# Toeplitz transfers from the diagonal on, with zeros written early, on the S5 stage of a one-core trunk kernel

## The reference

```
u      : 64 groups of 16 features
states : s[t] = lam_bar * s[t-1] + b_bar u[t]   (complex, 64 states a group)
y      = gelu(real(c s) + d * u)
y      = y * sigmoid(y @ glu_w + glu_b)         (1024 x 1024)
```

## Time and profile before

| what | us |
|---|---|
| median of 3 runs | 1279.68 (1279.62 to 1280.75) |
| the profiled execution | 1278.21 |
| its span | 1276.4 |
| start of the first GLU product in it | 101.61 |
| x load for the transposes: issue by SP, and time to landing | 50.39, 7.6 |
| POOL's last instruction ends | 78.4 |

### The profile page before, as it was taken

The page is one execution under the profiler, slowest core; times in us unless marked ns, Lnnn a source line. Parts: engine busy times, 40 slices in busy tenths (PEclk is TensorE's granted clock), DMA queues, the critical chain, the costliest instruction groups (busy, mean ns, idle before and its releaser), DMA issues.

```text
span 1276.4 us, 16013 instructions
## 1 busy us (share of the span) xinstructions
PE 1240.6 (97%) x6277; PEld 1034.5 (81%) x6277; DVE 671.7 (53%) x785; ACT 462.0 (36%) x486; POOL 64.8 (5%) x82
## 2 busy tenths in 40 slices
PE   3889999999999999999999999999999999999998
PEld 3778888888888888888888888888888888888886
DVE  8997754344444444646655465634454444444443
ACT  5635433333333333333333333422333333332232
POOL 6940000000000000000000000000000000000000
PEclk9999999999999999999999999999999999999999
DMA  5373333332312334323232133233232323323331
GB/s 115 100 144 123 99 99 99 99 99 90 105 58 90 105 90 138 107 66 107 66 99 83 57 107 96 69 96 93 74 119 80 102 94 99 99 68 90 93 110 66
DMA packets 141039, 121.03 MB, mean 95 GB/s; under 512 B 5720, under 2 KB 132880, under 8 KB 141008
## 3 DMA queue, kind: packets, MB, share of 16 engines
q1 hardware_dynamic: 138832, 116.40, 29.5%
q10 hardware_dynamic: 2176, 4.20, 1.7%
HBM read 114.29 MB, written 2.10 MB: 91 GB/s over the span
## 4 chain that ended last, share of the span: by engine, by line
PE 94%; ACTq 2%; ACT 2%; DMA 1%; DVE 1%; issue 0%; SPq 0%; DVEq 0%
PE bank L709 27%; PE bank L711 27%; PE bank L710 27%; PE bank L809 2%; PE bank L808 2%; PE bank L807 2%; ACTq L434 2%; DMA s<-in_x_dram 1%; PE bank L835 1%; PE bank L837 1%; PE bank L836 1%; PE bank L846 1%; PE bank L820 0%; PE bank L821 0%; ACT s_states L900 0%; PE bank L537 0%
## 5 line engine op out<-in xcount | busy, mean ns | idle before, releaser
L709 PE MATMUL bank<-u_hi,w_hi 128*128 128x512 f32 x960 | 374.9, 391 | 0.0
L711 PE MATMUL bank<-u_hi,w_lo 128*128 128x512 f32 x960 | 373.6, 389 | 0.0
L710 PE MATMUL bank<-u_lo,w_hi 128*128 128x512 f32 x960 | 373.5, 389 | 0.0
L1186 DVE TENSOR_TENSOR w_lo<-w_raw,w_hi 128x2048 fp32r<-128x2048 f32 x112 | 256.4, 2290 | 165.7 <-ACT w_hi L900 165.6
L900 ACT ACTIVATE w_hi<-w_raw 128x2048 fp32r<-128x2048 f32 x112 | 214.0, 1910 | 319.1 <-PE bank L711 314.0
L709 PEld LDWEIGHTS bank<-u_hi,w_hi 128*128 128x128 f32 x960 | 180.2, 188 | 37.8 <-issue 0.7
L710 PEld LDWEIGHTS bank<-u_lo,w_hi 128*128 128x128 f32 x960 | 180.2, 188 | 37.6 <-issue 0.5
L711 PEld LDWEIGHTS bank<-u_hi,w_lo 128*128 128x128 f32 x960 | 180.2, 188 | 37.5
L709 PE MATMUL bank<-h_hi,w_hi 128*128 128x512 f32 x352 | 136.9, 389 | 0.0
L710 PE MATMUL bank<-h_lo,w_hi 128*128 128x512 f32 x352 | 136.9, 389 | 0.0
L711 PE MATMUL bank<-h_hi,w_lo 128*128 128x512 f32 x352 | 136.9, 389 | 0.0
(11 more groups left out here) (220 smaller groups left out, 1321.6 us busy)
## 6 DMA issues: line engine op xcount, KB each, us to landing
w_raw<-in_ret_w_qkvg_dram SPq DMA_DIRECT2D x24, 1024.0 KB, 4.9
w_raw<-in_ffn_w_gate_dram SPq DMA_DIRECT2D x22, 1024.0 KB, 5.2
w_raw<-in_ffn_w_up_dram SPq DMA_DIRECT2D x22, 1024.0 KB, 5.1
w_raw<-in_ffn_w_down_dram SPq DMA_DIRECT2D x32, 704.0 KB, 4.1
w_raw<-in_ret_w_o_dram SPq DMA_DIRECT2D x8, 1024.0 KB, 5.1
w_raw<-in_s_glu_w_dram SPq DMA_DIRECT2D x4, 1024.0 KB, 5.5
s<-in_x_dram ACTq DMA_DIRECT2D x8, 256.0 KB, 8.5
s_w<-in_x_dram SPq DMA_DIRECT2D x1, 2048.0 KB, 7.6
```

The costliest lines, as they stand in the source:

```text
L709: pe.matmul(o, w_hi[w][:, w_cols], hi, start=first, stop=False)
L710: pe.matmul(o, w_hi[w][:, w_cols], lo, start=False, stop=False)
L711: return pe.matmul(o, w_lo[w][:, w_cols], hi, start=False, stop=end)
L1186: dve.tensor_tensor(w_lo[s][:, :], w_raw[:, s, :], w_hi[s][:, :].bitcast(F32), ALU.subtract).then_inc(w_lo_ready[s], 1)
```

## The change

Seven edits, all of them in the S5 stage:

- `strip` lies in the second half of `w_raw` only and holds the eight steps; sixteen partitions of the first half hold zeros (one memset by POOL).
- A Toeplitz transfer for r writes only the steps from r on: 8 - r steps instead of 8. The number of transfers stays.
- Seven transfers by SP, for r = 1 to 7, write the zeros of all parts and both halves, 16 partitions x 8 x r steps, from when the last transpose of `xn` is done.
- SP issues GLU piece 0 right after these have landed and the x load is issued, before its first Toeplitz part; piece 1 when all parts have landed.
- ACT splits piece 0 between the gelu table load and `strip_out(7)`.
- PE: `y_inputs(4)` before `y_states(0, 0)`; transposes 0 to 3 behind `y_inputs(7)`.
- `s5_input_out` goes through chunk, real or imaginary, j, with j innermost: it writes four floats in a row and reads PSUM with a stride, where it read in a row and wrote one float every 256 bytes.

```diff
-        strip = w_raw[0:4 * N, :, 0:(2 * STEPS - 1) * PART * N].rearrange("p s (t j n) -> p s t j n", t=2 * STEPS - 1, j=PART)
+        strip = w_raw[0:4 * N, 1, :].rearrange("p (s t j n) -> p s t j n", s=2, t=STEPS, j=PART)
+        zeros = w_raw[0:N, 0, 0:(STEPS - 1) * PART * N]
...
             for r in range(STEPS):
-                first = STEPS - 1 - r
-                queue.dma_start(toep[N * r:N * r + N, half, part, :, :, :].rearrange("p t j n -> p (t j n)"),
-                                strip[row:row + N, part % 2, first:first + STEPS, :, :].rearrange("p t j n -> p (t j n)")
+                queue.dma_start(toep[N * r:N * r + N, half, part, r:, :, :].rearrange("p t j n -> p (t j n)"),
+                                strip[row:row + N, part % 2, 0:STEPS - r, :, :].rearrange("p t j n -> p (t j n)")
                                 ).then_inc(toep_loaded[part], 16)
...
+            sp.wait_ge(zeros_set, 1)
+            b, fill = S5_AT[("u", 7)]
+            sp.wait_ge(bank_full[b], fill + 1)
+            for r in range(1, STEPS):
+                cols = r * PART * N
+                sp.dma_start(toep[N * r:N * r + N, :, :, 0:r, :, :].rearrange("p h q t j n -> p (h q) (t j n)"),
+                             repeated(zeros[:, 0:cols], 1, 2 * NPART)).then_inc(toep_zeroed, 16)
+
             b, fill = S5_AT[("tb", 4 * NTAB - 1)]
             sp.wait_ge(bank_full[b], fill + 1)
             sp.dma_start(x_tok, x[0].rearrange("(t p) d -> p t d", p=P)).then_inc(x_loaded, 16)
 
-            sp.wait_ge(pads_zeroed, 1)
+            sp.wait_ge(toep_zeroed, 16 * (STEPS - 1))
+            load_unit(0, 0, glu_v[:, :, 0:256], KT, 256)
             for part in range(NPART):
                 toeplitz_half(sp, part, 0)
-            for s in range(2):
-                for part in (s, 2 + s):
-                    sp.wait_ge(toep_loaded[part], 16 * 2 * STEPS)
-                load_unit(s, 0, glu_v[:, :, 256 * s:256 * s + 256], KT, 256)
+            for part in range(NPART):
+                sp.wait_ge(toep_loaded[part], 16 * 2 * STEPS)
+            load_unit(1, 0, glu_v[:, :, 256:512], KT, 256)
...
             pe.wait_ge(seg_done, 2)
-            y_states(0, 0)
             pe.wait_ge(toep_loaded[2], 16 * 2 * STEPS)
             y_inputs(4)
+            y_states(0, 0)
             y_inputs(5)
             y_states(1, 1)
-            for k in range(4):
-                y_transposed(k)
             pe.wait_ge(toep_loaded[3], 16 * 2 * STEPS)
             y_inputs(6)
             y_inputs(7)
+            for k in range(4):
+                y_transposed(k)
             y_states(2, 4)
             y_states(3, 5)
...
-                copy(states[:, 1:CH + 1, :, JB * SLOT[k]:JB * SLOT[k] + JB].rearrange("p c r j -> p j r c"),
-                     ps[:, :].rearrange("p (j r c) -> p j r c", j=JB, r=2)).then_inc(free, 1)
+                copy(states[:, 1:CH + 1, :, JB * SLOT[k]:JB * SLOT[k] + JB],
+                     ps[:, :].rearrange("p (j r c) -> p c r j", j=JB, r=2)).then_inc(free, 1)
...
             act.activation(small[:, 25:26], eps[:, :], ACT.Gelu_apprx_tanh)
+            split_weights(0, 0)
             strip_out(7)
             toeplitz_half(act, 3, 1)
...
-            split_weights(0, 0)
             for k in (4, 6, 5, 7):
                 gelu(k)
```

More of the change, by code:

```diff
@@ L354, in trunk @@
         tc_ready = sem("tc_ready")
-        pads_zeroed = sem("pads_zeroed")
+        zeros_set = sem("zeros_set")
+        toep_zeroed = sem("toep_zeroed")
         diag_ready = sem("diag_ready")
@@ L680, in y_inputs @@
                     pe.matmul(o, u[:, jj, half, :], toep[:, half, jj // PART, :, jj % PART, :], start=(jj % 4 == 0), stop=False)
+            pe.wait_ge(toep_zeroed, 16 * (STEPS - 1))
             pe.wait_ge(toep_loaded[0], 16 * 2 * STEPS)
@@ L960, in strip_out @@
                 rows32 = slice(2 * N * (k // 4), 2 * N * (k // 4) + 2 * N)
-                copy(strip[rows32, k % 4 // 2, STEPS - 1:, JB * (k % 2):JB * (k % 2) + JB, :],
+                copy(strip[rows32, k % 4 // 2, :, JB * (k % 2):JB * (k % 2) + JB, :],
                      ps[rows32, :].rearrange("p (j t n) -> p t j n", j=JB, t=STEPS)).then_inc(free, 1)
@@ L994, in _ @@
             strip_out(1)
-            act.wait_ge(pads_zeroed, 1)
             toeplitz_half(act, 0, 1)
@@ L1682, in _ @@
             pool.memset(fb[:, :, :, :], 0.0).then_inc(fb_zeroed, 1)
-            for s in range(2):
-                zeroed = pool.memset(strip[:, s, 0:STEPS - 1, :, :], 0.0)
-            zeroed.then_inc(pads_zeroed, 1)
+            pool.memset(zeros, 0.0).then_inc(zeros_set, 1)
             pool.wait_ge(ident_loaded, 16)
```

## The result

| kernel | median us | lowest to highest | runs | ratio to before, 95% interval |
|---|---|---|---|---|
| before | 1279.65 | 1277.23 to 1283.04 | 20 | |
| changed | 1283.41 | 1280.3 to 1285.56 | 20 | 1.0027 [1.0021, 1.0033] |

A forecast was written before the change was run, and what follows sets the result against it. Bound: ACT's Toeplitz chain, ending 1.5 us after DVE's scan, ahead of the first GLU product. Chain start -0.7, split +1.93, last block -0.3, landing -1.9, transposes +1.97: +1.0, 1280.7 us; range 1277.2 to 1283.2.

The forecast's parts named there:

- The likeliest case: ACT's chain as summed, clock kept: first GLU product at 102.6, +1.0 us, time 1280.7 us; chance 0.40.
- rival (a): TensorE's clock falls after PE's 4 us wait for part 3: y stage 1.5 us longer, 1282.2 to 1284; chance 0.27.
- What bounds the kernel; where the effect is read: PE is 97% busy; the change is worth what it moves the first GLU product, with 1174.8 us behind it.
- State copies at 605 ns, chain 0.7 earlier, scan 1.1 earlier: Copies fall from 1087 to 605 ns; ACT's Toeplitz chain starts 0.7 us earlier, DVE's scan ends 1.1 earlier.
- Weight split +1.93: On ACT, the moved split delays the last strip copy, last transfers and gelus: +1.93 us.
- Issues do not depend on size; landing 2.4 instead of 4.3: Toeplitz issues stay 0.61 us each; with 56% of the bytes the last landing shrinks, -1.9 us.
- Last block 5.8 us: ACT's last block of eight Toeplitz issues lasts 5.8 us, bounds 5.0 and 6.1; term -0.3.
- Transposes +1.97: On PE, transposes 0 to 3 no longer fill the wait for part 3, so y_inputs(7) comes first: +1.97 us.
- Zero transfers: cost nothing: SP's seven transfers take 19.5 us at worst; x lands at most 2.5 us later, unneeded until 62; bounds 0 and 0.5.
- (b): ACT's chain shortens as a whole, blocks near 5.0, part 3 at 90 or before; 1277.2 to 1279.5 us; chance 0.20.
- (d): Issue time goes with size, 0.4 us each, leaving the scan as floor: 1277.2 or 1276.5 us; chance 0.10.
- (c): Zeros or the GLU piece hold up x or SP's Toeplitz part 0: 1282 us or more; chance 0.03.

The follow-up runs named there:

- e4: The kernel before with the j-innermost state copies alone; 1278.49 us, ratio 0.9987 to before.
- e2: The changed kernel with the weight split back in its old place on ACT; 1280.04 us, ratio 1.0003 to before.
- e7: The changed kernel with full-length Toeplitz transfers of all eight steps (64 KB each); 1285.23 us, ratio 1.0039 to before.
- e11: The kernel before, full 64 KB transfers, with PE's new order alone (transposes 0 to 3 behind y_inputs(7)); 1284.01 us, ratio 1.0033 to before.
- e3: The changed kernel with both the weight split and PE's order of the transposes put back; 1280.36 us, ratio 1.0000 to before.
- e6: The changed kernel with each of the seven zero transfers cut to one step (448 instead of 1792 KB); 1280.92 us, ratio 1.0008 to before.
- e5: The changed kernel with four filler products on PE in its wait for Toeplitz part 3; 1281.69 us, ratio 1.0012 to before.
- e10: The kernel before with the j-innermost copies and three filler products on PE ahead of x's transposes; 1279.04 us, ratio 0.9997 to before.
- e1: The changed kernel with PE's old order of the transposes alone; 1282.12 us, ratio 1.0016 to before.
- e12: e10 with, in addition, half of ACT's last block of Toeplitz issues given to SP; 1279.25 us, ratio 0.9994 to before.

## Why the prediction was right, and where it was not

The direction held, and the time lies at the very end of the range, partly by luck. The range ended at 1283.2; the time is 1279.68 x 1.0027 = 1283.1 against the runs that were shown, and 1283.4 as the median of the twenty. The likeliest case, +1.0 us with the clock kept, was too small by 2.5 us: what came was rival (a), which was priced at 1282.2 to 1284.

In the changed kernel's trace the first GLU product starts at 106.08 where the sum had 102.6. These 3.5 us are three terms. The last issue block starts at 85.69 instead of 84.6 (1.1: the chain's early start was lost in the wait for x, and the second block began at 69.55 where 68.3 was implied). That block takes 6.87 us instead of 5.8 (1.1). From part 3 to the first GLU product it is 11.82 us instead of 10.47 (1.35: `y_inputs` 1.7 longer at the low clock, the last states 0.5 shorter). The steps:

- *What bounds the kernel; where the effect is read.* Right: 1174.8 us behind the first GLU product on both sides.
- *State copies at 605 ns, chain 0.7 earlier, scan 1.1 earlier.* The copies are right: 601 ns. Alone they made the kernel 1.6 us faster (e4), where 0.7 was summed. The 0.7 at the start of the chain could not be told: the changed kernel's trace has 1.65, e4's 0.13, and the spread between executions is as large.
- *Weight split +1.93.* Its size on ACT is right (1.90). On the kernel taking it back was worth 3.1 us, 1.6 to 4.6 by the intervals (e2). That the part above 1.9 is the clock behind a shorter wait fits the executions' granted clocks (median 0.996, changed kernel 0.995) and was not shown.
- *Issues do not depend on size; landing 2.4 instead of 4.3.* Right: e7, and 1.9 to 2.3 us.
- *Last block 5.8 us.* Mis-sized: 6.87, outside the bounds of 5.0 and 6.1. One of its issues took 1.91 us where the median is 0.61. What held it up is not shown; in the other traces this block of eight took 5.67 to 7.29 us, at either size.
- *Transposes +1.97.* Right in the sum and wrongly explained as a loss of its own. Old order: the gelus start when ACT's last issue is out, so the transposes cannot start earlier than 1.7 us behind it. With full transfers part 3 lands behind them, and they fill a wait: e11, 4.2 us. With short ones part 3 is there as early as the gelus, and no worth of the order is measured: e3, where 1.97 is at the edge of the intervals. The two terms, landing -1.9 and transposes +1.97, belong together: the first is there to be had only in the order that costs the second.
- *Zero transfers: cost nothing.* Wrong: this term was put at nothing, and e6, with a quarter of the zeros, is 2.4 us faster than the changed kernel. The rate was about right, but "at worst 19.5 us" was not a bound (32.5 to 53.6 is 21.1). x was to land at most 2.5 us later than 58.0, with PE's need at 62; in the changed kernel's trace it took 14.1 us, landed at 63.2, and PE waited for it. In the other traces with all zeros and x on SP's queue it landed at 59.7 to 60.8, nearly as bounded, and PE did not wait for it. So the cost is shown and its path is shown for one execution only; the rest stays open.
- *Clock, rival (a), chance 0.27.* This rival came, and the forecast's clock kept at full is the step that failed most clearly. PE was empty 5.35 us, the clock stood at 0.50 from 94.3 to 97, and e5 gives 1.9 us back where 1.5 was worked out. I had set it beside the forecast, though the nearer row spoke for it.
- *Rivals (b) and (d)* fell: part 3 was there at 94.3 and not at 90, and the median issue is 0.61 us at either size (e7). *(c)* was given 0.03; it came in the changed kernel's trace for x, and not for SP's part 0.

The effects do not add up one by one: split 3.1, clock 1.9, zeros 2.4 and copies -1.6 would be 5.8 for a measured 3.5. A likely reason is that the split and the zeros both lengthen a wait of PE behind which the clock falls, so that undoing either takes some of the clock's cost away as well. How much of each is the clock's was not separated, and each of the four numbers is uncertain by more than 1 us.

Two edits were not tried by themselves: the early GLU piece, and `y_inputs(4)` ahead of `y_states(0, 0)`. With the split and the order undone (e3) the kernel has the short transfers and the new copies and is still 1.7 us above e4, which has the copies alone (1.0000 against 0.9987, the intervals overlap a little). So nothing shows that short transfers and zeros together gain anything.

## What to carry to other kernels

Moving work "earlier" on an engine whose own instructions are the chain that ends last can cost its full length, however idle the place that it leaves (1.9 us on ACT here). Bytes written in advance are not free because the queue was empty: ask what is issued behind them and what that load's slack is, and measure with fewer of them. One trace of one execution names a path; look for it in a second kernel's trace before calling it the cause. And where a change lengthens an engine's wait on TensorE, price the wait and the clock behind it together; two edits that each fill or empty the same wait are to be summed as one.

## What the runs showed of the hardware

- Issuing a transfer of 16 partitions within SBUF takes 0.61 us on ACT and 0.59 on SP in the median, with 8 to 64 KB (changed kernel) as with 64 KB (e7). Single issues took up to 3.5 us, and a block of eight 5.0 to 7.3 us.
- The seven zero transfers, 1792 KB from 16 partitions to 16 partitions, took 21.1 us from the first issue to the last landing (changed kernel).
- Writes of four floats in a row cost ACT 601 ns for 512 columns (changed kernel), single floats at a pitch of 256 bytes 1087 (before).
- The granted clock fell behind or in waits of PE of 1.8 us (e10, at 82.8) to 5.6 us (e11). It stayed full behind one of 1.8 us in before (89.3), of 2.5 in e1 (62.5) and of 2.8 in e12 (94.4). So the length of the wait alone does not say whether it falls. Where PE was kept busy in a wait, it stayed full in the stretch behind (e5, e10, e12).
- The spread between executions goes with the clock. Of the 35 executions of before beside e1 to e4, the seven with a mean granted clock of 0.994 took 1281.1 us on average, the four with 0.999 took 1277.4. Executions of one kernel differ by 1.0 (e7) to 6.3 us (e1).
